# Down slabs split during the last pair, six plain tiles at the head, and two weight sums of each pair made by accumulating DMAs

## The reference, cut to what matters

```
def swiglu(x, w_gu, w_down):
    gate, up = jnp.split(x @ w_gu, 2, axis=-1)
    return (jax.nn.silu(gate) * up) @ w_down

def hybrid_layer(x, ...):
    h = layer_norm(DEEPNORM_ALPHA * x + 0.5 * swiglu(x, ffn1_w_gu, ffn1_w_down), ...)
    ...   # three mixer branches, gates, w_out
    h = layer_norm(DEEPNORM_ALPHA * h + merged @ w_out, ...)
    return layer_norm(DEEPNORM_ALPHA * h + 0.5 * swiglu(h, ffn2_w_gu, ffn2_w_down), ...)

def reference(...):
    x = first_block(...)      # hybrid_layer twice: four swiglu
    return second_block(x, ...)   # token mixer and a convolved FFN: plain products here
```

## Time and profile before

| what | us |
|---|---|
| median of 3 runs (3602.83 to 3608.93) | 3606.04 |
| the profiled execution | 3607.97 |
| its span, first to last instruction | 3606.1 |
| PE busy | 3515.3 |
| DVE busy | 2311.9 |
| ACT busy | 1692.5 |

### The profile page before, as it was taken

The page is one execution under the profiler, slowest core; times in us unless marked ns, Lnnn a source line. Parts: engine busy times, 40 slices in busy tenths (PEclk is TensorE's granted clock), DMA queues, the critical chain, the costliest instruction groups (busy, mean ns, idle before and its releaser), DMA issues.

```text
span 3606.1 us, 49977 instructions
## 1 busy us (share of the span) xinstructions
PE 3515.3 (97%) x19400; PEld 2950.5 (82%) x19400; DVE 2311.9 (64%) x4317; ACT 1692.5 (47%) x3259; POOL 0.2 (0%) x4
## 2 busy tenths in 40 slices
PE   9998999999999999999999999999999999999999
PEld 7898878877888987898888877888977677788887
DVE  6576656556785767576665566775766786666643
ACT  5354454554353545444555543553545443444432
POOL 0000000000000000000000000000000000000000
PEclk9999999999999999999999999999999999999999
DMA  3334331112323332323320112232323222233332
GB/s 129 100 103 138 114 93 34 45 48 68 97 85 103 94 114 67 106 90 116 88 71 27 48 59 85 94 102 80 118 64 106 66 65 88 74 94 94 94 94 70
DMA packets 170628, 308.52 MB, mean 86 GB/s; under 512 B 19030, under 2 KB 23287, under 8 KB 170392
## 3 DMA queue, kind: packets, MB, share of 16 engines
q1 hardware_dynamic: 169624, 304.54, 27.5%
q10 hardware_dynamic: 768, 0.79, 0.1%
HBM read 300.27 MB, written 4.72 MB: 85 GB/s over the span
## 4 chain that ended last, share of the span: by engine, by line
PE 90%; DVE 5%; ACT 3%; issue 1%; DMA 0%; SPq 0%; DVEq 0%; ACTq 0%
PE bank L2464 20%; PE bank L2473 20%; PE bank L2465 20%; PE bank L2499 6%; PE bank L2502 6%; PE bank L2501 6%; PE bank L2452 2%; PE bank L2447 1%; PE bank L2542 1%; PE bank L2635 1%; DVE w_lo L3209 1%; PE bank L2645 1%; PE bank L2510 1%; PE bank L2562 0%; DVE page_r L3262 0%
## 5 line engine op out<-in xcount | busy, mean ns | idle before, releaser
L2464 PE MATMUL bank<-page_r,w_hi 128*128 128x512 f32 (+1 forms) x3382 | 1363.5, 403 | 38.3 <-DVE w_lo L3209 31.0
L2473 PE MATMUL bank<-page_r,w_lo 128*128 128x512 f32 (+1 forms) x3382 | 1338.6, 396 | 0.0
L2465 PE MATMUL bank<-page_r,w_hi 128*128 128x512 f32 (+1 forms) x3382 | 1328.6, 393 | 0.0
L2464 PEld LDWEIGHTS bank<-page_r,w_hi 128*128 128x128 f32 x3382 | 640.9, 189 | 196.8 <-DVE w_lo L3209 35.1
L2787 ACT ACTIVATE w_hi<-raw 128x512 fp32r<-128x512 f32 x848 | 522.0, 626 | 593.5 <-PE bank L2473 588.9
L2473 PEld LDWEIGHTS bank<-page_r,w_lo 128*128 128x128 f32 x3382 | 639.9, 189 | 143.5
L2465 PEld LDWEIGHTS bank<-page_r,w_hi 128*128 128x128 f32 x3382 | 641.0, 190 | 140.1 <-issue 3.6
L3209 DVE TENSOR_TENSOR w_lo<-raw,w_hi 128x512 fp32r<-128x512 f32 x848 | 561.2, 685 | 130.8 <-ACT w_hi L2787 130.3
L2499 PE MATMUL bank<-page_r,w_hi 128*128 128x256 f32 x1904 | 539.1, 283 | 18.4 <-DVE w_lo L3241 12.1
L2502 PE MATMUL bank<-page_r,w_lo 128*128 128x256 f32 x1904 | 537.5, 282 | 0.0
L2501 PE MATMUL bank<-page_r,w_hi 128*128 128x256 f32 x1904 | 537.4, 282 | 0.0
(11 more groups left out here) (322 smaller groups left out, 3471.0 us busy)
## 6 DMA issues: line engine op xcount, KB each, us to landing
raw<-weights SPq DMA_DIRECT2D x848, 256.0 KB, 2.6
raw<-pairs SPq DMA_DIRECT2D x272, 256.0 KB, 2.7
page_f<-x_t SPq DMA_DIRECT2D x8, 256.0 KB, 5.3
bias_rows<-page_f SPq DMA_DIRECT2D x8, 256.0 KB, 2.0
page_f<-bias_rows SPq DMA_DIRECT2D x8, 256.0 KB, 2.7
out_t<-page_f SPq DMA_DIRECT2D x12, 128.0 KB, 1.8
cst<-consts SPq DMA_DIRECT2D x4, 272.0 KB, 5.2
page_f<-mem_t SPq DMA_DIRECT2D x8, 128.0 KB, 5.1
```

What stands on the lines that cost most here:

```text
L2464: self.e.matmul(o, hi, X.hi[kt], start=first, stop=False)
L2465: self.e.matmul(o, hi, X.lo[kt], start=False, stop=False)
L2473: last = self.e.matmul(o, lo, X.hi[kt], start=False, stop=final)
```

## The change

1. **Sums by DMA.** `prepare` loads a21 twice, into s1 and s3 (a pair of units), and then two DMAs of a new engine program, `Pool`, add a22 to s1 and a11 to s3 on their way (accumulate). POOL waits for the landing of the load, and each unit gets a second semaphore for the landing of the sum. `sum_bottom` is gone. a11, a12 and a22 are still loaded for themselves. So per pair: five loads of 256 KB by SP in place of four, and two accumulating DMAs of 256 KB by POOL. h13 and `sum_second` wait for the sums' landing.
2. **The end of a run of pairs.** `ahead` has six pieces in place of two. They are called inside the last pair's turn: after q1 load slabs s and s+1; before the next product load s+2; before q3 split slab s; before q2 load s+3, split s+1; at the end load s+4, split s+2. And the first four blocks of the first down product (`follow`) are placed between the last q7 and the last q4.
3. **ALONE = 6** in place of 5: six plain tiles, 16 pairs per FFN, 64 in all.

```
-NPAIR = 68
+NPAIR = 64
-ALONE = 5
+ALONE = 6
...
+        def add(part, unit):
+            below = unit.full
+            unit.adds += 1
+            unit.full = (unit.added, 16 * unit.adds)
+            self.add_part(p, part, unit, below)
+
         k = p.prep
-        a11, a21 = self.raws.take_pair()
+        out = s1, s3 = self.raws.take_pair()
+        load("a21", s1)
+        load("a21", s3)
+        yield
+        add("a22", s1)
+        add("a11", s3)
+        a11 = self.raws.take()
         load("a11", a11)
-        load("a21", a21)
         yield
         a12, a22 = self.raws.take_pair()
+        load("a12", a12)
         load("a22", a22)
-        load("a12", a12)
-        yield
-        out = self.raws.take_pair()
-        low, high = sorted((a11, a22), key=lambda u: u.at)
-        k.will(vector="bottom")
-        self.sum_bottom(p, low, high, a21, out)
-        self.raws.give(a21, k["bottom"])
-        s1, s3 = out if low is a22 else out[::-1]
         yield
         s2, s4 = self.raws.take_pair()
...
-        self.round_units(p, "h13", out, h13, [k["bottom"]])
+        self.round_units(p, "h13", out, h13, [s1.full, s3.full])
...
             if cur:
                 step(cur)
+                if not nxt:
+                    next(ahead)
                 self.pair_product(cur, "q5", cur.c, True)
...
+            if not cur:
+                for _ in range(SLAB):
+                    self.bg.tell(follow)
             if prev:
                 self.pair_product(prev, "q4", prev.b, False, prev.k["c22"])
+            if cur and not nxt:
+                next(ahead)
...
         def ahead(blocks):
             self.until(blocks)
             s = self.next_block // SLAB
-            for i in range(LOADED - 1):
-                self.loaded(s + i)
+            self.loaded(s + 1)
             yield
+            self.loaded(s + 2)
+            yield
+            self.rested(s)
+            yield
+            self.loaded(s + 3)
+            self.rested(s + 1)
+            yield
+            self.loaded(s + 4)
             self.rested(s + 2)
...
     def sum_second(self, p, s1, a11, s2):
         self.clear(s2)
-        self.wait_ge(*p.prep["bottom"])
+        self.wait_ge(*s1.full)
+        self.wait_ge(*a11.full)
...
+class Pool(Engine):
+    def add_part(self, p, part, unit, below):
+        self.wait_ge(*below)
+        self.e.dma_start(unit.f, self.m.pairs[p.number, QUARTERS.index(part)], accum_op=ALU.add) \
+            .then_inc(unit.added, 16)
```

More of the change, by code:

```diff
@@ L33 @@
 SLAB = 4
-NSLAB = 1120 - 4 * 68
-NPAIR = 68
+NSLAB = 1120 - 4 * 64
+NPAIR = 64
 NRAW = 14
@@ L151, with __init__ @@
 class Unit(Slot):
-    def __init__(self, region, rounded, at, landed):
+    def __init__(self, region, rounded, at, landed, added=None):
         super().__init__(region[:, at * UNIT:(at + 1) * UNIT], rounded[:, at * UNIT:(at + 1) * UNIT])
         self.at, self.region, self.rounded, self.landed, self.loads = at, region, rounded, landed, 0
+        self.added, self.adds = added, 0
     def wide(self):
@@ L464, in __init__ @@
         self.s_raw = [sem(f"slab_landed{i}") for i in range(NRAW)]
+        self.s_added = [sem(f"slab_added{i}") for i in range(NRAW)]
         self.s_hi, self.s_lo, self.s_gemm = sem("slab_rounded"), sem("slab_rest"), sem("blocks_multiplied")
@@ L487, in idle @@
         pass
-    load_part = sum_bottom = sum_second = sum_fourth = round_units = rest_units = pair_matmuls = idle
+    load_part = add_part = sum_second = sum_fourth = round_units = rest_units = pair_matmuls = idle
     pair_seed = pair_keep = pair_first = pair_gate = pair_lift = pair_join = pair_round = pair_rest = pair_last = idle
@@ L515, in __init__ @@
         self.banks = Stock([Slot(b) for b in memory.bank_aps])
-        self.raws = Units([Unit(memory.raw, memory.w_lo, i, memory.s_raw[i]) for i in range(NRAW)], LENT["raw"])
+        self.raws = Units([Unit(memory.raw, memory.w_lo, i, memory.s_raw[i], memory.s_added[i]) for i in range(NRAW)], LENT["raw"])
         self.his = Units([Unit(memory.w_lent, memory.w_hi, i, None) for i in range(NHI)], LENT["hi"])
@@ L746, in norm_of_norm, with update @@
         yield from self.rms_norm(X, name, after, stats.early, k["scale"])
-    def update(self, mat, H, scale, stats, tiles=8, k0=0, beside=None):
+    def update(self, mat, H, scale, stats, tiles=8, k0=0, beside=None, begun=None):
         if beside:
@@ L751, in update @@
         for m in range(tiles):
-            w = Later(self.product(mat, m, H, k0=k0))
+            w = begun if begun and m == 0 else Later(self.product(mat, m, H, k0=k0))
             while not w.done:
@@ L934, in prepare @@
         self.round_units(p, "h24", [s2, s4], h24, [k["fourth"]])
-        h1, h3 = h13 if out[0] is s1 else h13[::-1]
+        h1, h3 = h13
         p.units = {"q1": (h11, a11, k["l11"]), "q5": (h1, s1, k["l13"]), "q7": (h3, s3, k["l13"])}
@@ L961, in pair_product, with paired @@
         self.bg.now += 1.42
-    def paired(self, mat, js, X, H, head, ahead):
+    def paired(self, mat, js, X, H, head, ahead, follow):
         take = self.pages.take
@@ L1041, in paired @@
             step(later)
-            if not nxt:
+            if cur and not nxt:
                 next(ahead, None)
@@ L1046, in ffn @@
     def ffn(self, source, X, up, down, scale, early, after, scaled=None, mem=None):
-        H = Operand()
+        H = Operand(FIRST)
         pairs = [m for j in range(ALONE) for m in (j, FT + j)]
@@ L1092, in ahead @@
             s = self.next_block // SLAB
-            for i in range(LOADED - 1):
-                self.loaded(s + i)
+            self.loaded(s + 1)
             yield
+            self.loaded(s + 2)
[6 more added lines that the diff above has]
+            self.loaded(s + 4)
             self.rested(s + 2)
         head.step(until=6)
-        self.paired(up, range(ALONE, FIRST), X, H, head, ahead(FIRST * DT))
-        part, H = H, Operand()
+        follow = Later(self.product(down, 0, H))
+        self.paired(up, range(ALONE, FIRST), X, H, head, ahead(FIRST * DT), follow)
+        part, H = H, Operand(FT - FIRST)
         head = self.pair(up, FIRST, FT + FIRST)
@@ L1103, in ffn @@
         for m in range(DT):
-            w = Later(self.product(down, m, part))
+            w = Later(self.product(down, m, part)) if m else follow
             while not w.done:
@@ L1114, in ffn @@
         self.drop(part, w.value.full)
-        self.paired(up, range(FIRST, FT), X, H, head, ahead(NSLAB * SLAB))
+        follow = Later(self.product(down, 0, H, k0=FIRST))
+        self.paired(up, range(FIRST, FT), X, H, head, ahead(NSLAB * SLAB), follow)
         self.drop(X, (self.lanes["pair"].tensor, self.lanes["pair"].raised[0]))
-        return self.update(down, H, scale, Spread(self, after, after.count == 2), k0=FIRST, beside=mem)
+        return self.update(down, H, scale, Spread(self, after, after.count == 2), k0=FIRST, beside=mem, begun=follow)
     def project(self, mat, mt, X, n=512, product=None):
@@ L3852, in _ @@
             Vector(e, memory).run()
+        @block.gpsimd
+        def _(e):
+            Pool(e, memory).run()
     return plan.order, plan.pair_order
```

## The result

The changed kernel takes **3557.9 us** (median of 4 runs, 3556.5 to 3559.2) against 3605.2 for the kernel before in the same series (3602.8 to 3608.9): ratio 0.9868, 95% interval 0.9851 to 0.9885, or 47.3 us less. Forecast were 3566 and a range of 3558 to 3590: the forecast is 8 us too high, and the median lies just under its range. Its profiled execution took 3558.9 (span 3557.1), 49.1 less than the one that the forecast's sum was made on.

The account below looks back on a forecast made before the run. PE, busy 97% of the span, was taken to bound the kernel. From the profiled 3607.97 us, +5.0 (tiles), -18.3 (heads), -27.4 (ends) and 0 (DMA sums) gave 3567.3, from the median 3565.3; predicted 3566, range 3558 to 3590.

Parts of the forecast that it names:

- Six plain tiles, +5.0: Plain tiles of the FFNs: four pairs become plain, each tile 11.20 us against 9.94 for a turn, +5.0 us.
- Heads, -18.3: Starts of the pairs in FFN 2 to 4: late pairs and half clock go, since X sums end before the sixth tile, -18.3 us.
- 0.87: Head of pairs: loss by the fourth product in FFN 1, let stand at each head, 0.87 us.
- The end of a run, -27.4: Eight ends of runs of pairs: early loads and splits and four plain blocks remove both waits, -27.4 us.
- the 3.42 us: Each end of a run: delay between the last q7, q4 and first plain matmul beyond normal spacing, 3.42 us, taken eight times.
- Sums by DMA, 0: Turns of pairs: taking 1.22 us a turn off VectorE gains 0, if the sums land in time (8.7 us).
- A: Heads: they stay late, so the 18.3 is not won but the 5.0 is paid, 3584 us; chance 0.12.
- B: Ends of runs: they keep half their wait, some 1.7 us at each of eight, 3580 us; chance 0.08.
- C: h13 and sum_second each turn: accumulating DMA slower than 8.7 us, 3630 us at 11; chance 0.12 (0.09 slower than before).
- the 64 us: Turns of pairs: cost if a DMA sum takes 11 us, 1.15 us in each of 56 turns, +64 us.
- -40.7: Whole kernel: the forecast's net gain from tiles (+5.0), heads (-18.3) and ends (-27.4), 40.7 us.

Follow-up runs that it names:

- tiles_only: The kernel before with six plain tiles alone (ALONE = 6, NPAIR = 64): 3593.79 us, ratio 0.9968.
- ends_only: The kernel before with the change at the end of a run alone (early slab loads and splits, four plain blocks before the last q4): 3570.45 us, ratio 0.9905.
- dve_sums: The changed kernel with the sums by VectorE again, ends and six plain tiles as changed: 3560.4 us, ratio 0.9877.
- better1_dve: better1 with the sums by VectorE in place of the accumulating DMAs: 3553.44 us, ratio 0.9857.
- late_sums: The changed kernel, each accumulating DMA also waiting for the pair product last before it in order (q5): 3684.73 us, ratio 1.0227.
- dma_only: The kernel before with the two sums by accumulating DMAs alone: 3601.26 us, ratio 0.999.
- better1: The changed kernel with FFN 1 at five plain tiles, X sums skipped at every fifth block, head pair prepared to step 8: 3554.56 us, ratio 0.9862.
- better1_again: better1 unaltered, run again beside the changed kernel on one chip: 3552.52 us against 3558.86, ratio 0.9854.

## Why the prediction was wrong, and where it was right

*Six plain tiles, +5.0: right.* The sixth tile runs at 0.70 us a block and the pairs follow it after 0.23; turns of pairs stayed at 9.94.

*Heads, -18.3: the mechanism right, the size too great by 3.3.* The pauses of 4 us, the half clock and the wait for a11 went, 0.87 stayed at each. The step that failed: "The X sums [...] are now over when the sixth begins", from which I took that nothing else there is late. They were not: in FFN 2 the sixth tile begins at 1047.10, and the last operation of the X sums (L3277) runs on DVE behind that, with the slab rest that PE then waits for at 1050.50 directly after it:

```profile
1048.54 1.29 DVE L3277 SCALAR_TENSOR_TENSOR page_r<-page_f,page_r 128x512 fp32r<-128x512 f32 x2 [0.35 <-ACT page_r L2829]
1049.76 1.29 DVE L3235 TENSOR_TENSOR w_lo<-raw,w_hi 128x512 fp32r<-128x512 f32 x2
```

While they still ran they held up two slab rests, 0.33 and 0.43 us of idle time and from start to start 1.1 us an FFN, 3.3 in all; *tiles_only* shows the same two waits. FFN 1 of the kernel before, which I took as the model, had such a wait among its X sums, and by looking only at its fourth pair product I passed over it:

```profile
49.82 0.50 PE L2464 MATMUL bank<-page_r,w_hi 128*128 128x512 f32 x1 [0.51 <-DVE w_lo L3209]
```

*The end of a run, -27.4: the mechanism right, the size too small by some 8.* This is the step that put the forecast outside its range. The failing term is the 3.42 us. It is exact for what it counts, the time between the matmuls, and all eight ends have it. But I took it from FFN 2's end, which is one of three without half clock behind the pause, and multiplied by eight; at five ends the clock was at half behind the pause, and four blocks took up to half as long again (4.34 for 2.90 us). At the heads I had seen that and counted to the fourth product. At the ends I did not look past the first matmul. *ends_only* measured 34.7; 27.4 + 8 is 35.4.

*Sums by DMA, 0: right*, shown twice (*dve_sums*, *better1_dve*). DVE's `sum_second` waited for DMAs of quarters 30.3 us in 27 times; who waited for the sums alone stands below it (DVE 12.3 in 18, ACT 7.6 in 7), the rest was for the plain load of a11. Turns of 9.94 show that none of it reached PE:

```profile
DVE raw L3241 <- DMA raw<-pairs: 30.3, 27, 2.9
```
```profile
  DVE raw L3241: 12.3, 18
  ACT w_hi L2822: 7.6, 7
```

The DMA share came to 0.76 where I had put 0.65. By "SBUF — State Buffer" (Who interferes with whom) of the Trainium skill a tensor_tensor with both inputs in SBUF can hold up GpSimd's reads, but not, as the page infers, its making of descriptors. The trace agrees with the inference: POOL issued each sum in 0.86 us in median, 1.15 at most, while DVE was busy 7.56 of 10 us, and DVE's rests of 512 columns stayed at 0.69.

*The rivals.* A failed (heads lose 0.87; what I named for it, that DVE was seamless before that head, was misread, as DVE idles 0.70 us there at each activation), B failed (ends lose nothing), C failed with its premise: no sum took over 8.0 us. Its mechanism is real, as *late_sums* shows. By that run it would probably have cost more than the 64 us I gave it: there a first turn of a run pays 4.6 to 6.6 us more than in the changed kernel, three to four times the mean 1.65 of the others, and my 56 turns leave the first ones out.

*The sum again.* -40.7 + 3.3 - 8 = -45.4, against -47.3 between medians and -49.1 between the two profiled executions. That the forecast came within 8 us is in part luck: its two errors have opposite signs. By the traces the rest of the 49 lies in stages that the change leaves alone, 2.0 us between the second run of pairs of FFN 1 and the head of FFN 2, and 1.3 behind the second run of FFN 4. It is of the size of the spread of the runs (6 us between the four of the kernel before), and its cause was not looked for. Elsewhere than at heads and ends the two traces show nearly as much half clock, 31 us before and 27 after (without the last microseconds of each span).

**What stays open:** why the clock falls behind the same pause at some ends and not at others. It fell at 5 of 8 in the kernel before, 3 of 8 in tiles_only and 6 of 8 in dma_only, at other places each time. It fell at all three heads with a pause of 4 us in the kernel before and in *ends_only*, at two of the three with 2.9 in *dma_only*, and at none of sixteen ends with pauses of 1.9 and 0.9 us. The wait of 2.07 between FFN 3 and 4 is in every trace; the clock fell behind it in *tiles_only*, *dma_only*, *dve_sums*, *late_sums* and all three traces of the better versions, and stayed up in the other seven. Nor is it a matter of the kernel alone: *better1* and *better1_again* are the same program, and behind the same wait of 2.22 us the clock fell in the second and not in the first.

## What to carry to other kernels

A pause of the engine that bounds the kernel costs its idle time and what the clock does behind it, unless that engine then waits for another anyway, as at the heads of *dma_only*. Measure it from the last undisturbed instruction to one well behind the pause, and on every instance of the pattern: one of eight was read here, and it was one of the cheap ones. Work taken from an engine is worth what the bound waits for it, and no more: 1.22 us a turn off VectorE were worth 3.8 us in the kernel with late heads and nothing measurable in the one without. Where a transfer takes the place of an operation, work out its deadline in the first turn too, which has least room.

## What the runs showed of the hardware

An accumulating DMA of 256 KB from HBM into SBUF, issued by GpSimd, landed 4.0 to 8.0 us after its issue, 5.8 in median, with 0.86 us of GpSimd per issue; a plain load of the same size had 2.7 before and 3.3 beside the sums. So a sum took about as long as two plain loads, 5.4 to 6.6. By the fit that "DMA: Bandwidth & Descriptors" (Anatomy of one DMA) of the Trainium skill gives for a DMA of GpSimd, 2.0 us and 1 us more for each 436 KB, one plain DMA of this size is estimated at 2.6 us and two of them at 5.2, which is near; the plain loads measured here were issued by SP.

The sums by DMA cost VectorE nothing: its rests of 512 columns took 0.68 to 0.69 us with them as without.

The granted clock fell to its half behind waits of PE as short as 1.93 us, and did not behind others of 2.57; at an end with full clock on both sides four blocks took 2.90 us, at one with half clock 4.34.
